# One core, three chained transformer blocks: GLA head work reordered, the exp(-b) factor kept in SBUF, the convolution norm's steps packed two to a slot, lambda computed first

## The reference

```python
b = jnp.cumsum(logg, axis=2)
q_e = q * jnp.exp(b)
a = jnp.einsum('bnihd,bnjhd->bnhij', q_e, k * jnp.exp(-b))
a = jnp.where(tril(64, 64), a, 0.0)
o_intra = jnp.einsum('bnhij,bnjhv->bnihv', a, v)
k_dec = k * jnp.exp(b_last - b)
# step: o_c = q_c @ s;  s = dec_c * s + k_c^T v_c     (both directions)
hc = depthwise_conv(c1 * sigmoid(c2));  y_b = silu(layer_norm(hc)) @ w_o_conv
y = gates[0] * y_a + gates[1] * y_b + gates[2] * y_c;   return y @ w_out
```

## Time and profile before

| | us |
|---|---|
| median of 3 runs | 3658.07 |
| lowest, highest | 3656.41, 3661.84 |
| the profiled execution | 3658.07 |
| its span, first to last instruction | 3656.0 |
| PE busy | 3572.7 (98%) |
| ACT busy | 1264.2 |
| DVE busy | 1229.2 |
| POOL busy | 1525.4 |

### The profile page before, as it was taken

How to read it: one execution, slowest core, us unless ns; L and a number is a source line. 1 busy time by engine, 2 the same in 40 slices (tenths; PEclk the granted TensorE clock), 3 DMA queues, 4 the chain that set the end, 5 groups by cost and what they waited for, 6 DMA issues and landing times.

```text
span 3656.0 us, 39083 instructions
## 1 busy us (share of the span) xinstructions
PE 3572.7 (98%) x16100; PEld 2828.7 (77%) x16100; DVE 1229.2 (34%) x2095; ACT 1264.2 (35%) x1927; POOL 1525.4 (42%) x717
## 2 busy tenths in 40 slices
PE   8999999998999999999999999999999999999999
PEld 3777887877788888887677888888886778887766
DVE  3155684531221134211553111111114542112474
ACT  3433323432322333223444222322233443222543
POOL 2422354556344444455314444444454134443422
PEclk8999999999899999999999999999999999998999
DMA  6211133442233323333112233333331022332211
GB/s 224 92 53 52 54 110 103 156 145 86 87 130 137 97 99 132 136 101 99 43 32 87 98 97 95 97 98 95 92 102 64 29 75 92 98 91 88 75 41 52
DMA packets 98717, 341.17 MB, mean 93 GB/s; under 512 B 11307, under 2 KB 11563, under 8 KB 98124
## 3 DMA queue, kind: packets, MB, share of 16 engines
q1 hardware_dynamic: 97632, 334.02, 27.9%
q10 hardware_dynamic: 908, 4.67, 0.3%
HBM read 336.02 MB, written 2.10 MB: 92 GB/s over the span
## 4 chain that ended last, share of the span: by engine, by line
PE 92%; DVE 3%; ACT 3%; DMA 1%; POOL 1%; issue 1%; SPq 0%; DVEq 0%; ACTq 0%
PE ps L1116 25%; PE ps L1118 25%; PE ps L1117 24%; PE ps L1395 3%; PE ps L1419 2%; PE ps L1135 2%; PE ps L1136 2%; PE ps L1137 2%; PE ps L1406 1%; PE ps L1311 1%; PE ps L1325 1%; DVE t L2032 1%; PE ps L1190 1%; PE ps L1150 1%; PE ps L1397 1%
## 5 line engine op out<-in xcount | busy, mean ns | idle before, releaser
L2534 POOL TENSOR_TENSOR t<-t,t 128x1024 fp32r<-128x1024 f32 (+2 forms) x588 | 1358.0, 2311 | 1910.2 <-ACT t L1483 1909.4
L1116 PE MATMUL ps<-t,t 128*128 128x512 f32 (+1 forms) x4048 | 1614.5, 399 | 37.2 <-DVE t L2032 12.2
L1118 PE MATMUL ps<-t,t 128*128 128x512 f32 (+1 forms) x4048 | 1589.4, 393 | 0.0
L1117 PE MATMUL ps<-t,t 128*128 128x512 f32 (+1 forms) x4048 | 1584.4, 391 | 0.0
L1116 PEld LDWEIGHTS ps<-t,t 128*128 128x128 f32 x4048 | 767.7, 190 | 210.2 <-issue 19.8
L1118 PEld LDWEIGHTS ps<-t,t 128*128 128x128 f32 x4048 | 766.2, 189 | 168.3
L1117 PEld LDWEIGHTS ps<-t,t 128*128 128x128 f32 x4048 | 767.7, 190 | 157.1 <-issue 1.0
L1483 ACT CAST t<-t 128x1024 fp32r<-128x1024 f32 (+2 forms) x588 | 585.1, 996 | 594.3 <-PE ps L1118 394.3
L2336 DVE TENSOR_TENSOR t<-t,ps 128x512 f32<-128x512 f32 x110 | 75.6, 687 | 543.6 <-PE ps L1118 535.4
L1550 ACT CAST t<-t 128x512 fp32r<-128x512 f32 x158 | 97.1, 623 | 406.0 <-DVE t L2336 367.8
L1774 ACT ACTIVATE t<-ps,t 128x128 f32<-128x128 f32 (+3 forms) x160 | 84.1, 527 | 236.9 <-DVE t L2394 174.2
(11 more groups left out here) (275 smaller groups left out, 2475.6 us busy)
## 6 DMA issues: line engine op xcount, KB each, us to landing
t<-in_w_f1i SPq DMA_DIRECT2D x88, 512.0 KB, 3.4
t<-in_w_f2i SPq DMA_DIRECT2D x88, 512.0 KB, 3.3
t<-in_w_ada SPq DMA_DIRECT2D x72, 512.0 KB, 4.3
t<-in_w_ffi SPq DMA_DIRECT2D x44, 512.0 KB, 3.6
t<-in_w_f1o SPq DMA_DIRECT2D x32, 512.0 KB, 3.5
t<-in_w_f2o SPq DMA_DIRECT2D x32, 512.0 KB, 3.5
t<-in_w_gate SPq DMA_DIRECT2D x24, 512.0 KB, 3.4
t<-in_w_out SPq DMA_DIRECT2D x48, 256.0 KB, 2.7
```

What stands on the lines that cost most here:

```text
L1116: e.matmul(out, wh[:, at], X.hi[c][:, 0:N], start=c == first, stop=False)
L1117: e.matmul(out, wh[:, at], X.lo[c][:, 0:N], start=False, stop=False)
L1118: m = e.matmul(out, wl[:, at], X.hi[c][:, 0:N], start=False, stop=c == final)
L2534: e.tensor_tensor(k.WL[:, n % NHL, 0:w], k.raw[:, j % NRAW, 0:w], f(k.WH[:, n % NHL, 0:w]), ALU.subtract).then_inc(*k.rest.inc(('rest', j) ...
```

## The change

Seven edits:

- In a GLA head `decayed` is called three slots of `beside` later (behind `head_scale(0)`), and `masked` behind the two slots and `head_scale(1)` that stood behind it.
- The factor exp(-b) is written to `KE` in SBUF and multiplied there; before it was written back into the bank `suf`. `suf` is now freed by ACT. The activation for it comes first of the three.
- `modulations` has no empty step between a group's last sum and its close.
- The list `ln` has single steps only: squares are not in pairs and there are no empty entries. In the `su` loop one is taken for each unit as before, in the branch two for each slot.
- In the `oconv` branch `ada()` is called for j < 3, before for j < 5.
- `mix_lambda` is called ahead of the unit `ff`.

```diff
@@ first(): the GLA heads
         on.prepare(h, 1)
-        on.decayed(h)
         if h:
             on.head_scale(0, h - 1)
-        beside(6)
+        beside(3)
+        on.decayed(h)
+        beside(3)
         on.inner(h)
-        on.masked(h)
         if h:
             on.head_scale(1, h - 1)
         beside(2)
+        on.masked(h)
         on.chain_begin(h)
@@ first(): modulations()
                     on.ada_sum(name, g, kt)
                     yield
-                yield
                 on.ada_close(name, g)
@@ first(): the convolution's norm
-    ln = iter([[('mean', 0)]] + [[('center', i)] for i in range(KT)] + [[('square', i), ('square', i + 1)] for i in (0, 2, 4, 6)] + [[], [('roots', 0)], [], [('row', 0)]] + [[('apply', i)] for i in range(KT)])
-
-    def conv_norm():
-        for step in next(ln, ()):
-            on.conv_norm(*step)
+    ln = iter([('mean', 0)] + [(s, i) for s in ('center', 'square') for i in range(KT)] + [('roots', 0), ('row', 0)] + [('apply', i) for i in range(KT)])
...
-            conv_norm()
+            on.conv_norm(*next(ln))
...
-    def norm_ada(j):
-        conv_norm()
+    def conv_norm(j):
+        for _ in range(2):
+            on.conv_norm(*next(ln, ('', 0)))
         ada()
-    branch(on, 2, 'osgu', XA, k.SA, norm_ada)
+    branch(on, 2, 'osgu', XA, k.SA, conv_norm)
...
-    branch(on, 1, 'oconv', XA, k.CN, lambda j: ada() if j < 5 else None, done=mixture)
+    branch(on, 1, 'oconv', XA, k.CN, lambda j: ada() if j < 3 else None, done=mixture)
@@ second()
     on.mix_loads(L, last)
+    on.mix_lambda(L, layer)
     on.T(('ff', L), 'ff' + L, 0, A)
...
-    on.mix_lambda(L, layer)
@@ Scalar.prepare()
+        e.activation(k.KE[:, d, :], tri, ACT.Exp, scale=-1.0).then_inc(*k.act.inc(('k decay', h, d)))
         self.wait_ge('filled', ('suf', h, d))
-        e.activation(k.KD[:, d, :, :].rearrange('p a n -> p (a n)'), self.bank('suf', h, d), ACT.Exp).then_inc(*k.act.inc(('t decay', h, d)))
-        self.wait_ge('t decay', h, d)
-        e.activation(self.bank('suf', h, d), tri, ACT.Exp, scale=-1.0).then_inc(*k.act.inc(('k decay', h, d)))
+        e.activation(k.KD[:, d, :, :].rearrange('p a n -> p (a n)'), self.bank('suf', h, d), ACT.Exp).then_inc(*k.act.inc(('t decay', h, d), ('free', ('suf', h, d))))
@@ Vector.decayed()
-            if h:
-                self.wait_ge('filled', ('a', h - 1, d))
-            e.tensor_tensor(KE[:, d, :], self.bank('suf', h, d), K, ALU.mult).then_inc(*k.dve.inc(('ke', h, d), ('free', ('suf', h, d))))
+            e.tensor_tensor(KE[:, d, :], KE[:, d, :], K, ALU.mult).then_inc(*k.dve.inc(('ke', h, d)))
```

More of the change, by code:

```diff
@@ L548, in first @@
             on.spatial(i - LEAD)
-    def norm_ada(j):
-        conv_norm()
+    def conv_norm(j):
+        for _ in range(2):
+            on.conv_norm(*next(ln, ('', 0)))
         ada()
-    branch(on, 2, 'osgu', XA, k.SA, norm_ada)
+    branch(on, 2, 'osgu', XA, k.SA, conv_norm)
     for step in ln:
-        for s in step:
-            on.conv_norm(*s)
+        on.conv_norm(*step)
     YA = k.XA('y')
```

## The result

| | before | after |
|---|---|---|
| median, us | 3658.81 | 3744.5 |
| lowest, highest of 4 runs | 3656.41, 3661.84 | 3740.51, 3769.1 |
| ratio, 95% interval | | 1.024 (1.021 to 1.027) |
| profiled execution, its span | 3658.07, 3656.0 | 3736.0, 3733.9 |

Slower, as forecast, but by 86 us in the medians (78 in the profiled executions) where I had forecast 45; the time lies above my whole range (3676 to 3720). Over all 21 executions on record the changed kernel took 3731.7 to 3769.1 us. The heads, the branch and lambda cost time, as forecast; two further waits in the heads were not in the sum. One term was far too small, the clock.

What follows compares the result with a forecast made beforehand. TensorE, busy 3572.7 of 3656.0 us, was taken to bound the kernel; terms 0+0+12.2+23.2+0+4.2+5 gave +45 us on 3658.07, so 3703 us. The forecast case's own range was 3690 to 3716, with R1 and R2 3676 to 3720.

Steps and rivals of the forecast that it cites:

- (a): GLA heads: exp(-b) in SBUF costs 0, hidden by slack; by the port rule up to 2.4 us in one head.
- (b): GLA heads: decayed() three slots later costs 0 (-0.5 to +2 us), in heads 2 and 3 ending about when PE arrives.
- (c): GLA heads: later masked() frees banks late for PE's outer products, +4.3, +2.5, +2.8 and +2.6 us, sum +12.2.
- (d): Gate/osgu branch, convolution's norm: waits for roots, units 8 and 9 and ada_close, 31.1 us, net +23.2 us.
- one of my signs of being wrong: Branch: weight casts less than 9 us apart would show the forecast wrong.
- R1: Rival, branch: the apply loop does not stack, only the 12.2 us for the roots stay; 3684 us, chance 0.2.
- (e): Modulations: empty slot taken out and j < 3; 66 slots for 63 steps, closing directly costs 0.
- (f): Start of each mixing layer: mix_lambda ahead of 'ff' makes PE wait 3.55 us, twice; net +4.2 us.
- (g): Whole kernel: half clock behind waits, five new falls less two gone, 1.7 us each, +5 us (0 to +14).
- R2: Rival: half clock after each of ten new waits, exp(-b) products wait for POOL; +58, 3716 us, chance 0.1.

Runs made afterwards that it cites:

- e9_ke: The kernel before with only exp(-b) kept in KE in SBUF, decayed() in its old place: 3658.3 us, ratio 0.9998.
- e7_first: The kernel before with the `ln`, modulations and j < 3 edits, but ada() ahead of a branch slot's two norm steps: 3657.0 us, ratio 0.9997.
- e6_wide: e1_masked plus 24 useless wide matmuls behind the two first outer products of heads 0 and 2: 3700.6 us (3688 to 3715).
- e1_masked: The kernel before with only masked() moved behind head_scale(1) and the two slots of beside: 3698.1 us, ratio 1.0095.
- e5_filled: e1_masked plus useless matmuls ahead of the first and second outer products, where PE waits: 3678.9 us, ratio 1.0060.

## Why the forecast was off

- **(a) exp(-b) in SBUF, 0.** Right alone (e9_ke), wrong beside (b). The bound of 2.4 us a head held (1.5 and 1.7 measured), and I had the means to see it: I let the slack of head 0 in the earlier trace rows speak for heads 2 and 3, after saying in (b) that there the slack is gone.
- **(b) decayed() later, 0 (-0.5 to +2).** 2.8 us alone, above my bound, and 5.9 with (a). The step that failed is "decayed() ends about when PE arrives": it ended 1.0 and 1.1 us after PE came.
- **(c) masked(), +12.2.** 10.4 us of waits at the outer products: 3.7, 1.9, 2.7 and 2.0 in the four heads against 4.3, 2.5, 2.8 and 2.6. The step was right.
- **(d) the branch, +23.2.** Measured +24.7, by two errors that cancel: the closeness is luck. Waits 11.5 for the roots (forecast 12.2), 1.15 and 5.6 for units 8 and 9 (2.0, 5.8), 7.1 ahead of the close (11.1). The casts of slots 3 to 7 came 9.2, 11.2, 11.9 and 11.5 us apart (9.4, 10.2, 10.8 and 11.4 in the forecast). That of slot 8 came after 6.4 us, not 11.9, which was one of my signs of being wrong; why the loop did not hold this one is not shown. The last ada_sum even so ended at 796.3, within 0.6 us of the forecast (751.8 and the 45.1 from the heads). PE came later to the wait, since unit 9 began 1.9 us after its forecast time and took 1.7 us longer, partly at half clock. Waits +17.4, clock +7.3. R1 is refuted by the waits of 5.6 and 7.1 us; that the loop is made by the raw buffer, e7_first shows.
- **(e) modulations, 0.** It was not run apart from (d). e7_first, which has it too, is as fast as the kernel before.
- **(f) lambda, +4.2.** +9.6: waits 8.7 - 2.9 = 5.8, because the products were held beside POOL, and 3.8 of clock. The trace before had one such product of 0.99 us (L2342 at 2743.50, beside POOL), so the 0.15 each was not safe.
- **(g) the clock, +5 (0 to +14).** This is the term that failed: PE's busy time grew by 36 us. The forecast took "each time 1.7" from the earlier trace rows, where the matmuls behind the wait are wide, and applied it to two waits in front of the recurrence. Even the upper bound, and R2 with every new wait followed by 3.4 us, carried the same assumption: 13.6 us where the heads alone lost 31. An upper bound from rows, and an estimate: a step of the recurrence takes 3.87 us before (206.59 to 210.46) and 7.05 us at half clock after (366.52 to 373.57), so eight steps can lose 25 us in a head; 9.5 and 15.9 were lost in heads 0 and 2.

The trace before held a warning that I passed over. Its stretches at 0.50 are not all of 3.4 us:

```profile
908.70:932.40 23.70, 16.40 (x36) 9.87 (x37) 11.64 (x18) 8.13 (x11) 2.37 (x1) 0.50 0.00 1
...
3362.80:3393.50 30.70, 23.66 (x64) 16.61 (x65) 14.14 (x28) 13.95 (x22) 0.50 (x1) 0.50 0.07 26
```

There PE waits again and again (busy 16.4 of 23.7 us), so they are no twin of the recurrence. But they rule out 3.4 us as the length that every fall has.

## What to carry to other kernels

Price a new wait of TensorE with a wide range for the clock, and look at what stands behind it. Ahead of wide matmuls 2.5 to 3 us of idle time cost 3 to 5 us here. Ahead of the recurrence, waits of 3.7 and 2.7 us cost 13.2 and 18.6 us in heads 0 and 2 (9.5 and 15.9 of it clock), and waits of 1.9 and 2.0 us cost 4.2 and 2.8 in heads 1 and 3. Take the upper bound from the length of the run behind the wait, not from stretches seen elsewhere. When two edits each use the same slack, price them together. And in a loop that passes buffers, put the instruction that frees the buffer ahead of the work that merely shares the slot.

## What was not expected of the hardware

- PE, busy without a gap, stayed at half clock for 33.9 us (0.50, 33.90 of 33.90 us busy), while the same instructions run at full clock when no wait stands ahead of them (0.99 over the heads before). The Trainium skill (TensorE: Matmul & The Clock Gate, section "HAM oscillation — how this bites in real kernels") lays such losses to waits longer than any of those in the heads; here waits of 2.8 and 0.9 us in head 0, and of 2.7 us in head 2, were enough.
- The same wait of 2.7 us was followed by 34 us at half clock in head 2 of the changed kernel and by none in e6_wide; in head 1 the same waits were followed by 3.4, 10.2 and 30.5 us in three kernels. What sets whether the clock falls, and for how long, stays open. Half clock costs nothing where PE would have waited anyway (unit 9).
- One kernel's runs spread by 30 us (e1_masked), and those of the changed kernel by 37, when the long stretches are in it, and by 3 us when PE's waits are filled (e5_filled). A single run of such a kernel says little.
- A product of one column on DVE, 0.15 us as a rule, took up to 1.22 us beside POOL's addition.
